# Opening of a hybrid GLA/Fourier diffusion layer: modulation weights read first, tokens normed, turned and split tile by tile

## What is computed

```python
mod = silu(c) @ w_ada + b_ada               # 6 x 1024 values per token kind: shift, scale, gate (mixer, MLP)
h = rmsnorm(x, g_pre_mix) * (1 + scale) + shift
z = h @ w_in                                # columns q | k | v | g | low-rank fwd | low-rank bwd | u
y = concat(GLA(q, k, v, decay(low-rank), g), Fourier(u)) @ w_out
x = x + gate * rmsnorm(y, g_post_mix)
x = x + gate2 * rmsnorm(relu(h2 @ w_fc1)**2 @ w_fc2, g_post_mlp)     # h2: as h, from the new x
```

## Time and profile before

| | |
|---|---|
| median of three runs | 1362.85 us (1360.29 to 1365.71) |
| profiled execution | 1363.83 us, span 1362.0 us |
| mean granted TensorE clock | 0.956 |
| TensorE busy | 1254.5 us, 92% of the span |
| VectorE, ScalarE, GpSimd busy | 754.6, 425.8, 220.3 us |
| DMA | 97.26 MB, 71 GB/s over the span |

### The profile page before, as it was taken

One profiled execution on the slowest core, in us unless ns is written; L12 is line 12 of the kernel. 1 busy time (PEld: TensorE's weight loads), 2 busy tenths in 40 slices (PEclk: granted clock), 3 DMA queues, 4 the chain that ended last, 5 costly groups with the idle time before them and its releaser, 6 DMA issues.

```text
span 1362.0 us, 18776 instructions
## 1 busy us (share of the span) xinstructions
PE 1254.5 (92%) x7365; PEld 740.1 (54%) x7365; DVE 754.6 (55%) x1148; ACT 425.8 (31%) x736; POOL 220.3 (16%) x344
## 2 busy tenths in 40 slices
PE   2669999999977689989999999999999999999995
PEld 2435668887666354445655645545546456455442
DVE  2574575695468657875545453544444454535438
ACT  3464353322223346554311311303213113113013
POOL 1100000331122101213112111111111121111104
PEclk7789999999888799999999999999999999999998
DMA  9942112335321510111111011010112111110103
GB/s 257 289 167 62 32 32 71 98 124 187 101 88 32 201 32 0 32 31 32 63 32 63 31 47 48 31 63 31 63 32 63 31 63 31 50 44 32 32 0 139
DMA packets 70752, 97.26 MB, mean 71 GB/s; under 512 B 3077, under 2 KB 53386, under 8 KB 70666
## 3 DMA queue, kind: packets, MB, share of 16 engines
q1 hardware_dynamic: 70666, 96.04, 22.4%
HBM read 86.33 MB, written 9.70 MB: 71 GB/s over the span
## 4 chain that ended last, share of the span: by engine, by line
PE 52%; DVE 1%; ACT 1%; issue 1%; POOL 1%; POOLq 0%; ACTq 0%; DVEq 0%
PE bank L1161 52%; ACT gex L824 1%; DVE region L2129 0%; POOL small L739 0%; DVE region L2100 0%; POOL small L688 0%; DVE region L2022 0%; DVE ghb L2022 0%; ACT whi L565 0%; DVE region L2131 0%; DVE region L2011 0%; POOL small L737 0%; ACT region L1074 0%; ACT region L1079 0%; DVE region L2037 0%
## 5 line engine op out<-in xcount | busy, mean ns | idle before, releaser
L1161 PE MATMUL bank<-whi,region 128*128 128x512 f16 (+1 forms) x1872 | 487.2, 347 | 1.6 <-DVE region L1978 1.6
L1161 PE MATMUL bank<-region,whi 128*128 128x384 f16 (+1 forms) x1872 | 458.9, 328 | 12.9 <-issue 6.6
L1161 PE MATMUL bank<-wlo,region 128*128 128x512 f16 (+1 forms) x936 | 325.1, 347 | 0.0
L1161 PE MATMUL bank<-region,wlo 128*128 128x384 f16 (+1 forms) x936 | 306.4, 327 | 0.0
L1161 PEld LDWEIGHTS bank<-whi,region 128*128 128x128 f16 x1872 | 184.1, 98 | 162.1 <-issue 2.6
L1161 PEld LDWEIGHTS bank<-region,whi 128*128 128x128 f16 (+1 forms) x1872 | 183.1, 98 | 137.5 <-issue 11.4
L2100 DVE SCALAR_TENSOR_TENSOR region<-bank,small,region 128x512 f32<-128x512 f32 x144 | 106.7, 749 | 180.5 <-PE bank L1161 180.2
L1161 PE MATMUL bank<-region 128*128 128x512 f16 (+8 forms) x802 | 174.1, 383 | 7.9 <-DVE region L573 3.3
L565 ACT ACTIVATE whi<-stage,small 128x2048 f16<-128x2048 f32 (+1 forms) x42 | 82.3, 1960 | 304.0 <-PE bank L1161 291.1
L2085 DVE TENSOR_TENSOR region<-region 128x384 f32<-128x384 f32 x96 | 53.5, 557 | 189.9 <-ACT region L1129 189.8
L1161 PEld LDWEIGHTS bank<-region 128*128 128x128 f16 (+4 forms) x802 | 110.5, 169 | 60.6 <-issue 12.5
(11 more groups left out here) (156 smaller groups left out, 886.6 us busy)
## 6 DMA issues: line engine op xcount, KB each, us to landing
stage<-in_w_fc SPq DMA_DIRECT2D x32, 1024.0 KB, 5.3
stage<-in_w_ada SPq DMA_DIRECT2D x16, 1024.0 KB, 5.7
region<-in_w_ada SPq DMA_DIRECT2D x8, 1024.0 KB, 14.1
stage<-in_w_in SPq DMA_DIRECT2D x8, 1024.0 KB, 5.9
x_with_position<-region SPq DMA_DIRECT2D x9, 512.0 KB, 5.5
region<-x_with_position SPq DMA_DIRECT2D x9, 512.0 KB, 8.8
out_dram<-region SPq DMA_DIRECT2D x9, 512.0 KB, 2.6
region<-in_x_sample SPq DMA_DIRECT2D x8, 512.0 KB, 12.3
```

Source lines behind the costliest of these rows:

```text
L1161: return nc.tensor.matmul(out, lhsT, rhs, start=start, stop=stop, skip_group_check=True)
```

## The change

The modulation chunks, with the LR and Q chunks behind the second of them, are read ahead of all but three x tiles; the K and first u chunks are read ahead of the stores of x. Position rows are no longer read spread out: TensorE spreads two of 16 rows over a tile (`spread_pos`), VectorE adds them, and GpSimd adds the column half. The modulation is made as rows: `mod_spread` spreads a scale chunk with its bias over 128 partitions for both token kinds, and VectorE multiplies it by the norm gain (`gain_rows`); shift chunks stay two rows. `first_scale` sets the scale of h from these. Each x tile is then multiplied once by its factor and the gain (`gain_x`), and turned by products with the identity into which the shift enters as two f16 rows (`turn_h`); ScalarE and VectorE read both parts straight from the PSUM bank (`high_h`, `low_h`). The LR and Q products stand between the turns, block by block (`opening`). The vectors' rows stay in `vrow`, and the ones matrix has a tensor of its own.

In the diff, lines are moved left, and some lines are left out.

```diff
-start = []
-for what in "x0 a0 x1 a1 x2 x3 a2 x4 a3 x5 x6 a4 x7 x8 a5 a6 a7".split():
...
+arrivals = [(s[0], int(s[1])) for s in "x0 a0 a1 w0 w1 a2 a3 x1 a4 a5 x2 a6 a7 x3 x4 x5 x6 x7 x8".split()]
+EARLY = 3
+b_keys += [("gain", h) for h in range(2)]
+for what, n in arrivals:
+    if what == "x" and 1 <= n < EARLY:
...
+opening = []
+uses = [("z", 0, 0, 0), ("z", 1, 0, 0), ("z", 1, 1, 0), ("z", 0, 0, 1), ("z", 1, 0, 1), ("z", 1, 1, 1),
+        ("z", 0, 0, 2), ("z", 1, 0, 2), ("z", 1, 1, 2)]
+for n in range(EARLY, EARLY + 3):
+    opening.append(("pos", n))
+for n in range(NT):
+    if EARLY + 3 + n < NT:
+        opening.append(("pos", EARLY + 3 + n))
+    opening.append(("xT", n))
+    if n >= 2 and n - 2 < 6:
+        opening.append(uses[n - 2])
+opening += uses[6:]
+for key in opening:
+    if key[0] == "xT":
+        b_keys += [("xT", key[1], h) for h in range(2)]
     else:
-        b_keys.append(("mod", ada1[n]))
+        a_keys.append(key)
...
-for what, n in start:
+sp.dma_start(posr, a["k_pos_row"]).then_inc(s_pos, 16)
+sp.dma_start(posc, a["k_pos_col"]).then_inc(s_pos, 16)
+for what, n in arrivals:
     if what == "x":
-        if n % 2 == 1:
-            load_pos(n)
         load_x(n)
-    elif what == "rows":
+    elif what == "a":
         load_ada(n)
-    if (what, n) == ("x", NT - 1):
-        load_chunk(sp, 0)
-load_chunk(sp, 1)
+    else:
+        load_chunk(sp, n)
+load_chunk(sp, 2)
+load_chunk(sp, 3)
 sp.dma_start(ghb[:], a["g_head"][0].rearrange("h v -> (h v)").partition_broadcast(P)).then_inc(s_misc, 16)
...
+def add_columns(j):
+    pool.wait_ge(s_x[j], 16)
+    nc.gpsimd.tensor_tensor(x1[:, j, 512:D], x1[:, j, 512:D], posc, ALU.add).then_inc(s_posp, 1)
 def x_rstd(j):
     pool.wait_ge(s_ssq, 2 * (j + 1))
-    rstd(rst[:, j:j + 1], sqs[:, j:j + 1], ssq[:, 2 * j:2 * j + 2], D, s_rst)
-for j in range(NT):
+    rstd(rst[:, j:j + 1], sqs[:, j:j + 1], ssq[:, 2 * j:2 * j + 2], D, None)
+def x_factor(j):
+    nc.gpsimd.tensor_tensor(rsh[:, j:j + 1], rst[:, j:j + 1], hscl[0], ALU.mult).then_inc(s_rst, 1)
+pool.wait_ge(s_pos, 32)
+for j in range(EARLY):
+    if j >= 1:
+        add_columns(j)
     x_rstd(j)
+pool.wait_ge(s_hsc, 1)
+for j in range(EARLY):
+    x_factor(j)
+add_columns(EARLY)
+add_columns(EARLY + 1)
+for j in range(EARLY, NT):
+    if j + 2 < NT:
+        add_columns(j + 2)
+    x_rstd(j)
+    x_factor(j)
...
-    B.take(act, ("xT", j - 2, 1))
-nc.scalar.activation(xh[j % 2], x1[:, j, :], ACT.Copy, scale=rst[:, j:j + 1]).then_inc(s_xh, 1)
...
-square_x(1)
-for what, n in start:
-    if what == "x":
-        if n + 2 < NT:
-            square_x(n + 2)
-        if n + 1 < NT:
-            norm_x(n + 1)
...
+def high_h(j):
+    for h in range(2):
+        bank = B.take(act, ("xT", j, h))
+        nc.scalar.activation(HTh[:, 4 * h:4 * h + 4, P * j:P * j + P],
+                             bank[:].rearrange("p (k t) -> p k t", k=4), ACT.Copy).then_inc(s_th, 1)
...
+for what, n in arrivals:
+    if what == "x" and n < EARLY:
+        square_x(n)
+    elif what == "a":
         mod_part(n, ada1[n])
-chunk_high(act, 0)
...
-own.did(nc.scalar.activation(xT[:, k, toks], xT[:, k, toks], ACT.Identity,
-                             scale=amul[0][:, c:c + 1], bias=shf[0][:, c:c + 1]))
...
-        nc.scalar.activation(HTh[t_], xT[t_], ACT.Copy).then_inc(s_th, 1)
+    elif what == "w":
+        chunk_high(act, n)
+act.wait_ge(s_hsc, 1)
+for n in range(len(ada1) // 2):
+    act.wait_ge(s_shr, n + 1)
+nc.scalar.activation(shift_h, shift, ACT.Copy, scale=hscl[0][0:2, :]).then_inc(s_shh, 1)
+square_x(EARLY)
+square_x(EARLY + 1)
...
+at = 0
+for j in range(NT):
+    high_h(j)
+    if EARLY + 2 + j < NT:
+        square_x(EARLY + 2 + j)
+    if j >= 4:
+        evac_open(uses[at])
+        at += 1
+for key in uses[at:at + 3]:
+    evac_open(key)
+chunk_high(act, K)
+for key in uses[at + 3:]:
+    evac_open(key)
+for i in range(K, G_A):
     chunk_high(act, i + 1)
-    if i == LR:
-        for key in z_uses(i):
...
-elif i == K:
+if i == K:
     decay_logs(0)
...
+def spread_row(out, row, start, stop):
+    n = out.shape[0]
+    return mm(out, ident[0:R_ALL, row:row + 1].to_broadcast([R_ALL, n]), vrow[0:R_ALL, :], start, stop)
...
+def spread_pos(j):
+    bank = A.open(pe, ("pos", j))
+    rows = pos_pick[:, 2 * j - 2:2 * j, :].rearrange("p r t -> p (r t)")
+    mm(bank[:], rows, posr, True, True).then_inc(A.filled(("pos", j)), 1)
...
+def mod_spread(n, c):
...
+key = ("mod", c)
+bank = B.open(pe, key)
+row = R_BIAS + 8 * c[1] + 2 * c[2]
+if c[1] == SH_M:
+    mm(bank[0:2, 0:CW], sel2, part[n % 2][:], True, False)
+    for m in range(2):
+        ins = spread_row(bank[0:2, P * m:P * m + P], row + m, False, m == 1)
+else:
+    for v in range(2):
+        mm(bank[:, CW * v:CW * v + CW], sel2[:, v:v + 1].to_broadcast([P, P]), part[n % 2][:], True, False)
+        for m in range(2):
+            ins = spread_row(bank[:, CW * v + P * m:CW * v + P * m + P], row + m, False, m == 1)
+ins.then_inc(B.filled(key), 1)
...
-turn(("xT", n, h), xh[n % 2][:, 512 * h:512 * h + 512], lambda: pe.wait_ge(s_xh, n + 1))
...
+for what, n in arrivals:
+    if what == "x" and 1 <= n < EARLY:
+        spread_pos(n)
+    elif what == "a":
         mod_rows(ada1[n])
-    else:
-        mod_out(n, ada1[n])
+        if n >= 1:
+            mod_spread(n - 1, ada1[n - 1])
+        if n == 2:
+            sum_peaks(("w", 0))
+            sum_peaks(("w", 1))
         if n == 5:
-            sum_peaks(("w", 0))
-sum_peaks(("h", 0))
+            sum_peaks(("h", 0))
+mod_spread(len(ada1) - 1, ada1[-1])
...
+def turn_h(j):
+    pe.wait_ge(s_xh, j + 1)
+    v = 1 if j == 0 else 0
+    for h in range(2):
+        key = ("xT", j, h)
+        bank = B.open(pe, key)
+        for k in range(4):
+            d = slice(512 * h + P * k, 512 * h + P * k + P)
+            mm(bank[:, P * k:P * k + P], xg[:, j % 4, d], ident, True, False)
+            if j == 0 and h == 0 and k == 0:
+                pe.wait_ge(s_shh, 1)
+                pe.wait_ge(s_shl, 1)
+            mm(bank[:, P * k:P * k + P], shift_h[:, d], pick[:, v, :], False, False)
+            ins = mm(bank[:, P * k:P * k + P], shift_l[:, d], pick[:, v, :], False, True)
+        ins.then_inc(B.filled(key), 1)
...
-for i in range(G_A):
+pe.wait_ge(s_wlo, 2)
+for key in opening:
+    if key[0] == "pos":
+        spread_pos(key[1])
+    elif key[0] == "xT":
+        turn_h(key[1])
+    else:
+        _, i, m, t = key
+        B.wait_read(pe, ("xT", 3 * t + 2, 1))
+        up_tile(key, 0, i, m, t, HTh, HTl, 2 * RANK if i == LR else P).then_inc(A.filled(key), 1)
+        if key == ("z", LR, 0, 2):
+            sum_peaks(("w", 2))
+logits(0)
+for i in range(K, G_A):
     pe.wait_ge(s_wlo, i + 1)
...
-    if i == LR and n == 1:
-        sum_peaks(("w", 1))
-    if n == (2 if i == LR else 3):
+    if i == K and n == 1:
+        sum_peaks(("w", 3))
+    if n == 3:
         sum_peaks(("w", i + 2))
-if i == Q:
-    logits(0)
...
+def add_rows(j):
+    bank = A.take(dve, ("pos", j))
     dve.wait_ge(s_x[j], 16)
-    dve.wait_ge(s_pos[(j - 1) // 2], 48 if j <= 2 else 32)
-    own.did(V.tensor_tensor(x1[:, j, 0:512], x1[:, j, 0:512], posr[:, j - 1, :], ALU.add))
-    V.tensor_tensor(x1[:, j, 512:D], x1[:, j, 512:D], posc, ALU.add).then_inc(s_posd, 1)
...
+def gain_rows(c):
+    bank = B.take(dve, ("mod", c))
+    cs = slice(CW * c[2], CW * c[2] + CW)
+    if c[1] == SH_M:
+        V.tensor_copy(shift[:, cs], bank[0:2, 0:CW]).then_inc(s_shr, 1)
+        V.tensor_reduce(shift_peak[0:2, c[2]:c[2] + 1], bank[0:2, 0:CW], AX_X, ALU.max,
+                        apply_absolute_value=True).then_inc(B.read(("mod", c)), 1)
+        B.wait_read(dve, ("mod", c))
+        if c[2] == D // CW - 1:
+            V.tensor_reduce(shift_peak[0:2, 0:1], shift_peak[0:2, :], AX_X, ALU.max).then_inc(s_hmx, 1)
+    else:
+        if c[2] == 0:
+            for h in range(2):
+                B.wait_read(dve, ("gain", h))
+        V.scalar_tensor_tensor(out=gain[:, :, cs], in0=bank[:].rearrange("p (v n) -> p v n", v=2), scalar=1.0,
+                               in1=gain_row[:, cs].unsqueeze(1).to_broadcast([P, 2, CW]),
+                               op0=ALU.add, op1=ALU.mult).then_inc(B.read(("mod", c)), 1)
+        B.wait_read(dve, ("mod", c))
+        own.did(V.tensor_reduce(gain_peak[:, c[2]:c[2] + 1], gain[:, :, cs], AX_XY, ALU.max,
+                                apply_absolute_value=True))
...
+def first_scale():
...
+V.tensor_copy(gain_peak[:, 4:5], peak_sum).then_inc(s_pkr, 1)
+own.settle()
+dve.wait_ge(s_pkr, peak_no["h", 0] + 1)
+step(V.tensor_reduce(hinv[0], gain_peak[:, 0:4], AX_X, ALU.max))
+step(V.tensor_scalar(hinv[0], hinv[0], gain_peak[:, 4:5], D ** 0.5 / TOP, ALU.add, ALU.mult))
+step(V.tensor_scalar(hinv[0], hinv[0], TINY, None, ALU.max))
+V.reciprocal(hscl[0], hinv[0]).then_inc(s_hsc, 1)
...
+def gain_x(j):
+    dve.wait_ge(s_rst, j + 1)
+    if j >= 4:
+        B.take(dve, ("xT", j - 4, 1))
```

(104 more changed lines are left out.)

157 lines of the change are left out of this document (55 added, 102 removed).

## The result

The changed kernel takes **1430.46 us** (median of four runs, 1428.54 to 1436.79) against 1363.26 for the kernel before in the same comparison: a ratio of 1.051, 95% interval 1.0476 to 1.0544. That is slower, as forecast, but by 67 us and not by 11, and 39 us above the range. The profiled execution is the slowest of the four, 1436.79 (span 1435.0, mean clock 0.944).

What follows compares the result with a forecast made beforehand. The opening was taken to bound the kernel: TensorE runs from K through u and v without a gap, so K's start moves the end. Terms -14.1 + 21.7 + 3.1 = +10.7 gave 1374.5, less 1.0: 1373.5 us; range 1358 to 1391.

Steps and rivals of the forecast that it cites:

- Leg 1: Opening transfers: without position-row broadcasts and with six x tiles moved back, the last modulation chunk lands at about 38 us, not 62.
- Leg 2: From weights to the scale of h: the scale stands at 53.2 us instead of 67.3, 14.1 us gained.
- ScalarE's order: Early opening: high parts of the first two weight chunks precede the third modulation chunk's copy, ending at 31.6 for rows ready at 22.2.
- rival C: Opening: the scale keeps pace with the transfers, copies not held up, and stands at 44 us; time 1364; chance 0.11.
- Leg 3: From scale to K's start: 76.9 us, with nine turns by products at 3.06 us each; 21.7 us lost.
- Leg 4: Inside K: the u chunk's split and decay logarithms delay emptying the first bank, so K's fifth tile waits; 3.1 us lost.
- B: Opening: TensorE at half clock for half of the turns and a sixth of the products; time 1393; chance 0.16.
- E: Turns: a product with the identity costs twice as much, 72 blocks at 0.22 more, 16 us; time 1390; chance 0.02.
- A: Turns: they cost as the transposes do, 2.0 us a tile; time 1364; chance 0.18.
- the gates' price: TensorE: a 128-column f32 matmul takes 0.22 us at full clock, read from four starting at 483.94, the next at 484.83.

## Why the prediction was wrong

Against its own sum (1374.5 for the profiled execution) 62.3 us are missing: 48.1 in K's start, 3.2 from K to v and 11.0 behind v's first copy.

- **Leg 1 held.** Rates of 336 and 398 GB/s where the slow spells were.
- **Leg 2 held**: the scale at 54.8 for 53.2 (53.7 to 55.9 in the versions that share this front), and ScalarE's order held the copies up as I had worked out; rival C is out. Its gain was overrated all the same: against openings of before that stand at 62.7 to 67.3 it is 8 to 12.5 us, not 14.
- **Leg 3 failed, at one term**: "two f16 products with two rows each. Those have no row", priced at 0.08 between a 384-column product and a weight load. The price is right for a product among its own kind (0.07 in groups) and for 128 rows (a block of 0.39). But both bounds came from products of full height, and the term left out what two rows do to the products next to them. It missed 38.2 us between the scale and K: 17 in the spacing and, by difference, 21 in the clock.
- The rest of leg 3 was close. With 128-row products K starts at 138.9 for my 130.1. Of the 8.8, 0.5 is the scale's and 1.1 comes before the first turn, where the low part of the shift row took 2.28 us for 1.28; the first turn with the position row behind it, mostly at half clock, took 6.5 us for 4.0 (57.81 to 64.29), and the logits 8.0 for 4.3: VectorE added their bias behind the maximum of the u chunk (the wait of 1.64), and half clock followed.
- **Leg 4 held in its wait**, 3.07 for 3.1, and the run that splits the chunk in time confirms its cause. Half clock around it, which I left out, makes it 6.3 from K to v. The 11 us behind v were not in the sum, which took it that the end moves by as much as K does (K moved by 55.7, the span by 73.0); since delays alone show 4 to 11, I can't put them down to the change.
- **The rivals.** B named the place and the suspect (thin row products, half clock) but priced half of the turns; the first three, the ends of the later six and parts of the products ran at half clock. It should have been likelier than 0.16, since it was the one case in which an operation without a row set both its own price and the clock's. E had the size, 0.22 a block more, by a wrong mechanism: types may alternate freely. A was excluded by the gates' price, rightly.
- **The range** took no case in which B and a dearer block come together, though both hang on the same unpriced operation.

## What to carry to other kernels

Price a product by its rows as well as by its columns: where a short operand (a bias, two shift rows, sixteen position rows) is multiplied in between products of full height, fill it up with zeros to 128 rows, which cost nothing that shows here and gave back 33 us, or group the short ones, which gave back 23. Transfers that become faster help only as far as the engines behind them keep their clock. And when an operation has no row in the trace, let its unknown price move the rivals together rather than one at a time.
